# Gated recurrence of a mixer block: level factors as a tree of multiplied gates, paired value products, same-token term by head sums

## The reference: what is computed

```python
def step(S, inp):
    k_c, i_c, lf_c = inp[:3]
    g = jnp.cumsum(lf_c, axis=2)
    g_last = g[:, :, -1:, :]
    inter = jnp.einsum('bhtk,bhkv->bhtv', q_c * jnp.exp(g), S)
    rel = jnp.exp(jnp.where(causal, g[:, :, :, None, :] - g[:, :, None, :, :], -jnp.inf))
    scores = jnp.einsum('bhtk,bhsk,bhtsk->bhts', q_c, k_c, rel)
    o = inter + jnp.einsum('bhts,bhsv->bhtv', scores, i_c)
    S = (jnp.exp(g_last[:, :, 0, :])[..., None] * S
         + jnp.einsum('bhsk,bhsv->bhkv', k_c * jnp.exp(g_last - g), i_c))
    return S, o
```

## Time and profile before

| what | value |
|---|---|
| median of 3 runs | 5863.41 us (5860.79 to 5869.21) |
| the profiled execution, its own time | 5861.68 us |
| its span | 5859.9 us |
| granted TensorE clock, mean | 0.941 |
| busy: TensorE / VectorE / ScalarE / GpSimd | 5131.7 / 3377.3 / 1904.2 / 1745.5 us |

### The profile page before, as it was taken

One profiled execution on the slowest core, in us unless ns is written; L12 is line 12 of the kernel. 1 busy time (PEld: TensorE's weight loads), 2 busy tenths in 40 slices (PEclk: granted clock), 3 DMA queues, 4 the chain that ended last, 5 costly groups with the idle time before them and its releaser, 6 DMA issues. The chain is left out here.

```text
span 5859.9 us, 127569 instructions
## 1 busy us (share of the span) xinstructions
PE 5131.7 (88%) x55385; PEld 3930.2 (67%) x55385; DVE 3377.3 (58%) x5097; ACT 1904.2 (32%) x3020; POOL 1745.5 (30%) x1387
## 2 busy tenths in 40 slices
PE   6899999899995666587999868999988999989989
PEld 1588888788885555366888634444466788776667
DVE  2236656344444666576798257888864300058877
ACT  1234444233232443134211224444421300026652
POOL 2201111445453554034100005776743411100012
PEclk8999999899998888798999978999998999979999
DMA  5434434211112010464332421000055311230035
GB/s 200 124 107 163 150 135 152 95 56 60 60 52 90 23 58 27 159 215 146 96 108 94 164 101 41 17 17 23 14 176 160 99 68 69 78 127 39 32 116 165
DMA packets 430428, 568.20 MB, mean 97 GB/s; under 512 B 66918, under 2 KB 318694, under 8 KB 417214
## 3 DMA queue, kind: packets, MB, share of 16 engines
q1 hardware_dynamic: 362200, 380.35, 20.8%
q10 hardware_dynamic: 52470, 122.50, 5.5%
q0 software_dynamic: 15216, 57.44, 2.5%
HBM read 357.07 MB, written 203.12 MB: 96 GB/s over the span
## 5 line engine op out<-in xcount | busy, mean ns | idle before, releaser
L157 PE MATMUL p_bank<-p_hT_high,p_w_high 128*128 128x512 f32 (+1 forms) x2744 | 1037.0, 378 | 8.4 <-PEq L37 7.9
L159 PE MATMUL p_bank<-p_hT_high,p_w_low 128*128 128x512 f32 (+1 forms) x2744 | 1028.9, 375 | 0.0
L158 PE MATMUL p_bank<-p_hT_low,p_w_high 128*128 128x512 f32 (+1 forms) x2744 | 1028.7, 375 | 0.0
L157 PEld LDWEIGHTS p_bank<-p_hT_high,p_w_high 128*128 128x128 f32 x2744 | 517.0, 188 | 110.3 <-issue 17.6
L159 PEld LDWEIGHTS p_bank<-p_hT_high,p_w_low 128*128 128x128 f32 x2744 | 516.7, 188 | 93.7
L158 PEld LDWEIGHTS p_bank<-p_hT_low,p_w_high 128*128 128x128 f32 x2744 | 517.2, 188 | 91.4
L2902 POOL TENSOR_TENSOR at_acc<-at_acc,at_p 128x512 f32<-128x512 f32 x256 | 414.7, 1620 | 123.2 <-ACT at_p L2838 100.9
L2838 ACT ACTIVATE at_p<-at_sc 128x1024 f32<-128x1024 f32 (+1 forms) x296 | 284.5, 1012 | 377.6 <-PE at_sc L2729 368.9
L1560 PE MATMUL rsc_db<-rsc_W,rsc_TK 64*64 64x64 f32 x8640 | 383.1, 219 | 4.3 <-issue 3.8
L2944 DVE TENSOR_REDUCE at_mx<-at_mb 128x2 f32<-128x1024 f32 (+1 forms) x280 | 342.0, 1221 | 51.2 <-PE at_mb L2740 50.9
L157 PE MATMUL o_bank<-o_w_high,o_m_high 128*128 128x512 f32 x800 | 315.0, 394 | 62.6 <-POOL o_m_low L151 62.6
(11 more groups left out here) (433 smaller groups left out, 10575.0 us busy)
## 6 DMA issues: line engine op xcount, KB each, us to landing
rsc_X<-rwkv_chunks SPq DMA_DIRECT2D x108, 320.0 KB, 4.5
pT<-p_o ACTq DMA_DIRECT2D x128, 256.0 KB, 2.2
rwkv_chunks<-p_arr POOLq DMA_DIRECT2D x54, 512.0 KB, 5.3
o_z<-pT SPq DMA_DIRECT2D x50, 512.0 KB, 5.3
o_y<-y SPq DMA_DIRECT2D x50, 512.0 KB, 6.7
pT<-p_eo ACTq DMA_DIRECT2D x96, 256.0 KB, 2.0
x<-o_o ACTq DMA_DIRECT2D x32, 512.0 KB, 2.7
o_x<-x SPq DMA_DIRECT2D x32, 512.0 KB, 4.7
```

What stands on the lines that cost most here:

```text
L157: nc.tensor.matmul(out, lhs[0], rhs[0], start=start, stop=False)
L158: nc.tensor.matmul(out, lhs[0], rhs[1], start=False, stop=False)
L159: return nc.tensor.matmul(out, lhs[1], rhs[0], start=False, stop=stop)
```

## The change

It replaces running sums and their exponentials by products of gates. f = sigmoid(z) is the gate itself, `products(p, j)` the products of blocks of 2**j gates. The asks qe start as q times f and the keys ke as sigmoid(-z); at each level a copy of the later half of qe and of the earlier half of ke goes out to LVL (ScalarE), and then the same halves are multiplied in place by the product of the block that lies between (VectorE for asks, GpSimd for keys). After six levels qe and ke are the factors that the state term and the state need. Keys and values are turned three units ahead into one of five buffers, the values twice over, so that two levels' scores, side by side on 128 rows, meet the values in one product. The same-token term of both directions is v times the head sum of q times (k of direction 0 plus k of direction 1), made once per channel tile in the two context units of direction 1. The state term and the value products share one PSUM bank and one output operation. Gates are double-buffered, and the reset mask of the scan is not loaded any more. The diff, cut to its core (semaphore waits for reused buffers are left out in places):

```diff
-def hgrn(nc, PT, q0, i0, z0, seg, masks, ident, YH):
+def hgrn(nc, PT, q0, i0, z0, masks, ident, head_ones, YH):
...
-    MC = (LV + 1) * HD
+    LEAD, NK = 3, 5
+    PAIRS = LV // 2
+    MC = 2 * PAIRS * HD
...
-        KI = [s.sb(f"KI{u}", [P, 2, P]) for u in range(3)]
+        KI = [s.sb(f"KI{u}", [P, 3, P]) for u in range(NK)]
...
+        def side(a, j):
+            x = (a + j) % 2
+            return slice(x * HD, (x + 1) * HD)
+        def spot(a, j):
+            x = a * PAIRS + j // 2
+            return slice(x * HD, (x + 1) * HD)
...
             def _(pool):
+                def key_step(p, w, j):
+                    r = region(PHASES[p][1], w)
...
+                        pool.wait_ge(k_step[w], LV * p + j)
+                        pool.wait_ge(block_step, LV * p + j)
+                    if w < 2:
+                        pool.wait_ge(k_level[w], LV * p + j + 1)
+                    _, early = halves(ke[p % 2][:, r], 2 ** j, PHASES[p][1])
+                    nc.gpsimd.tensor_tensor(early, early, factors(p, j, r)[0], ALU.mult).then_inc(k_step[w], 1)
+                def same(p):
+                    m = PHASES[p][0]
+                    x = k[p % 2][:, 0:SEQ]
+                    pool.wait_ge(k_ready, p + 1)
+                    nc.gpsimd.tensor_tensor(x, x, k[1 - p % 2][:, 0:SEQ], ALU.add).then_inc(k_summed, 1)
+                    pool.wait_ge(k_summed, m + 1)
+                    nc.gpsimd.tensor_tensor(x, x, q[m % 2][:], ALU.mult).then_inc(same_ready, 1)
...
+                for p in range(NP):
                     for j in range(LV):
+                        key_step(p, 1, j)
                     if p + 1 < NP:
+                        for j in range(LV):
+                            key_step(p + 1, 2, j)
+                        if PHASES[p + 1][1]:
+                            same(p + 1)
+                        for j in range(LV):
+                            key_step(p + 1, 0, j)
...
             def _(act):
+                    nc.scalar.activation(ke[p % 2][:], f[p % 2][:], ACT.Sigmoid, scale=-1.0).then_inc(ke_raw, 1)
+                    nc.scalar.activation(k[p % 2][:, 0:SEQ], f[p % 2][:, 0:SEQ], ACT.Sigmoid, scale=-1.0).then_inc(k_ready, 1)
+                    nc.scalar.activation(f[p % 2][:], f[p % 2][:], ACT.Sigmoid).then_inc(f_ready, 1)
+                def level(p, w, j):
...
+                    nc.scalar.copy(early, keys).then_inc(k_level[w], 1)
+                    act.wait_ge(q_step[w], (LV + 1) * p + j + 1)
+                    nc.scalar.copy(late, asks).then_inc(q_level[w], 1)
...
                 for g in range(NU):
+                    if g + LEAD < NU:
+                        turned(g + LEAD)
+                    if unit(g)[4] < NLT and unit(g)[3] == 0:
+                        keep(g)
+                    if n < LV:
+                        level(p, 1, n)
                     if p + 1 < NP:
                         if n == 1:
+                            raw_keys(p + 1)
                         if n == 3:
+                            keep_keys(p + 1)
+                        if n == 4:
+                            gates(p + 1)
+                        if 9 <= n < 9 + LV:
+                            level(p + 1, 0, n - 9)
...
             def _(dve):
+                def blocks(p, j):
...
+                    nc.vector.tensor_tensor(out, late, early, ALU.mult).then_inc(block_step, 1)
+                def first_asks(p, w):
...
+                    nc.vector.tensor_tensor(qe[p % 2][:, r], q[m % 2][:, r], f[p % 2][:, r], ALU.mult).then_inc(q_step[w], 1)
+                def ask_step(p, w, j):
...
+                    nc.vector.tensor_tensor(late, late, factors(p, j, r)[1], ALU.mult).then_inc(q_step[w], 1)
...
+                    nc.vector.tensor_tensor(k[p % 2][:, t], yb[:, i % 2, :], v[m % 2][:, t], ALU.mult).then_inc(same_evac, 1)
...
+                    nc.vector.tensor_tensor(Y[w][:], Y[w][:], k[p % 2][:, w * HALF:(w + 1) * HALF], ALU.add).then_inc(same_added, 1)
...
                 for g in range(NU):
                     p, n = divmod(g, CH)
                     if g + 1 < NU:
                         state(g + 1, 0)
                         if unit(g + 1)[4] < NLT:
                             mask(g + 1)
                         state(g + 1, 1)
+                    if unit(g)[4] < NLT and unit(g)[3]:
+                        add(g)
+                    if unit(g)[3] and n < NCX:
+                        times_v(p, 2 * n)
+                        times_v(p, 2 * n + 1)
+                        add_same(p, n)
+                    if n < LV:
+                        ask_step(p, 1, n)
+                    if p + 1 < NP:
+                        if n == 6:
+                            for j in range(1, 3):
+                                blocks(p + 1, j)
+                        if n == 7:
+                            for j in range(3, LV + 1):
+                                blocks(p + 1, j)
+                            first_asks(p + 1, 0)
+                        if n == 8:
+                            first_asks(p + 1, 1)
+                        if 9 <= n < 9 + LV:
+                            ask_step(p + 1, 0, n - 9)
...
             def _(pe):
-                    nc.tensor.transpose(tb[:, 0, 0:P], ke[p % 2][:, t], idn[:])
-                    nc.tensor.transpose(tb[:, 1, 0:P], v[m % 2][:, t], idn[:]).then_inc(t_prod, 1)
+                    for a in range(2):
+                        chunk, ra = slice(c * P + a * HD, c * P + (a + 1) * HD), slice(a * HD, (a + 1) * HD)
+                        nc.tensor.matmul(tb[g % 2][ra, 0:P], ke[p % 2][:, chunk], idn[:], start=True, stop=True)
+                    for a in range(2):
+                        chunk = slice(c * P + a * HD, c * P + (a + 1) * HD)
+                        for x in range(2):
+                            last = nc.tensor.matmul(tb[g % 2][x * HD:(x + 1) * HD, (1 + a) * P:(2 + a) * P], v[m % 2][:, chunk], idn[:], start=True, stop=True)
...
+                            nc.tensor.matmul(yb[rh, a, 0:HD], S[(2 * g + i) % 6][rh, :], qe[p % 2][rh, t:t + HD], start=True, stop=False)
+                def back(g):
+                    pe.wait_ge(pr_ready, latents(g + 1))
+                    for i in range(PAIRS):
+                        for a in range(2):
+                            for h in range(2):
+                                rh = slice(h * HD, (h + 1) * HD)
+                                last = nc.tensor.matmul(yb[rh, a, 0:HD], KI[g % NK][:, 1 + a, rh], PR[g % 2][:, h, spot(a, 2 * i)],
+                                                        start=False, stop=(i + 1 == PAIRS))
...
+                    for h in range(2):
+                        rh = slice(h * HD, (h + 1) * HD)
+                        last = nc.tensor.matmul(yb[rh, i % 2, :], ones[:, rh], k[p % 2][:, i * NT:(i + 1) * NT], start=True, stop=True)
...
                 for g in range(NU):
-                    if g + 2 < NU:
-                        turn(g + 2)
                     if g + 1 < NU:
                         front(g + 1)
+                    if unit(g)[4] < NLT:
+                        asked(g)
+                    if g + LEAD < NU:
+                        turn(g + LEAD)
+                    if unit(g)[3] and unit(g)[1] < NCX:
+                        for i in range(2):
+                            same(unit(g)[0], 2 * unit(g)[1] + i)
                     if unit(g)[4] < NLT:
                         back(g)
```

379 lines of the change are left out of this document (161 added, 218 removed).

## The result

The changed kernel takes **5737.4 us** in the median of 4 runs (5732.4 to 5747.6), the kernel before 5866.3 beside it: ratio **0.9781 [0.9769, 0.9793]**, 2.2% faster. Forecast was 5764, range 5722 to 5822: the time is in the range, 27 us under the forecast.

What follows compares the result with a forecast made beforehand. TensorE was taken to be bound by instruction supply, 256 per 3.95 us. First value product at 1889 plus 371 us (units 96 x 3.4, seams 13 + 15 + 9 + 8) ends at 2260, 98.6 us less: 5764 us, range 5722 to 5822.

Steps and rivals of the forecast that it cites:

- Instruction supply bounds TensorE: Gated recurrence, kernel before: TensorE's instructions arrive in blocks of 256, one per 3.95 us; a unit costs 4.07 us.
- Supply still sets the pace, with little to spare: Changed kernel's latent units: a block takes 3.66 us of TensorE work against 3.95 us of supply.
- rival C: Units with a rung: ScalarE, GpSimd and VectorE form a chain, 72 units at 4.1 us, 50 us back, 5814 us; chance 0.14.
- The pace of a unit: Latent units of the stage: 3.4 us each, 96 units, from 3.13 by supply plus small waits; bounds 2.9 and 4.07.
- GpSimd's passes: Two 4.6 us GpSimd passes for the head sums hold VectorE's first asks: 3 us x 3 = 9 us.
- No gain of their own: Scan, masked exponentials and all but one table load, removed by the change: costed at no gain, being hidden.
- for shorter seams I take nothing: Granted clock, 0.50 over the start and 0.89 over the rest: no gain counted from shorter seams.
- Start: From the first loads to the first value product: it comes at 1889 instead of 1919.4, bounds 1886 to 1899.
- Seams: Five changes of phase: 13 us for context units, 15 for head sums, 9 for GpSimd passes, 8 for late gate loads.
- A: TensorE's stops belong to the unit, not the record count: pace 4.1, 67 us given back, 5831 us; chance 0.12.
- B: Supply is hidden with fewer records; pace is TensorE's own 2.9 us, 48 us less, 5716 us; chance 0.10.
- D: Units with a rung: the same chain wholly serial, 5.2 us a rung, 130 us given back, 5894 us, slower; chance 0.04.

Runs made afterwards that it cites:

- before_light: Kernel before, elementwise work preparing a phase cut to a sixteenth of its columns from the third phase on, all TensorE instructions kept: 5833.3 us, ratio 0.9940.
- before_lean: Kernel before with 12 of 28 value products of a unit left out, 215 TensorE instructions in place of 263: 5843.7 us, ratio 0.9962 to the kernel before.
- halved: Kernel after with each value product made in two of 32 columns, 251 instructions a unit: 5785.3 us, ratio 0.9865 to the kernel before.
- small_rungs: Kernel after with level work of GpSimd, VectorE and ScalarE cut to a sixteenth of its columns from the second phase on: 5710.3 us, ratio 0.9728.
- z_early: Kernel after with the gates of the next two phases loaded ahead of the output's stores: 5733.3 us, ratio 0.9777 to the kernel before.
- split_same: Kernel after with GpSimd's two 2048-column sums cut into eight 512-column operations between its key products: 5731.2 us, ratio 0.9768 to the kernel before.
- late_asks: Kernel after with VectorE's ask steps issued one unit later, ahead of the output's add: 5732.9 us, ratio 0.9774 to the kernel before.
- best1: Kernel after with split_same, z_early and late_asks together: 5734.2 us, ratio 0.9779 to the kernel before.
- filler: Kernel after with fifteen one-column products a unit added into unused columns, 263 instructions: 5823.1 us, ratio 0.9927 to the kernel before.

## Why the prediction was right, and where not

**Instruction supply bounds TensorE: right for the kernel before.** In the stretches where little else holds it, 256 instructions took 3.92 us (before, from restart to restart), 3.92 and 3.85 (before_light), 3.71 (before_lean, sixth phase), 3.93 (halved), 3.83 and 3.74 (small_rungs), and 3.81 between restarts of the kernel after and of small_rungs, whether a unit asks for 263, 251, 215 or 203. My 3.95 is the upper end of that.

**"Supply still sets the pace, with little to spare": wrong for the kernel after.** My sign for it, stops every 256 records, did not come: 5 stops with 5.8 us are left. "Issue" fell from 37.1 to 2.4 us at the scores because a unit asks for 203 instructions in place of 263, and at 3.23 us a unit that is one block in 4.07 us, slower than blocks come. What stands above the own unit of 2.71, 47 us in 90 intervals, is for the most part waits for VectorE and ScalarE (35.1 us in the table of waits, with those at the seams). VectorE is busy for 24.23 of the 26.64 us of the first window here. So 3.4 came near to the measured pace partly by luck: I had it from supply and small waits, and what holds the kernel after is closer to the chain of rival C, weaker than priced there. Windows of the kernel after, second and sixth phase:

```profile
1977.21:2003.85 26.64, 24.13 (x866) 22.35 (x864) 24.23 (x50) 10.31 (x20) 10.04 (x11) 1.00 0.07 24
2208.84:2234.74 25.90, 24.91 (x900) 23.21 (x898) 14.57 (x38) 3.83 (x8) 0.00 (x0) 1.00 0.07 24
```

3.94 and 3.69 us for 256; the first is not supply's, since no stop lies in that window. The Trainium skill (Runtime: NRT & Kernel Launch, section Instruction fetch mechanics) has fetch hidden; the 61 stops of the kernel before and the 22 of small_rungs, 16.5 us at 203 instructions a unit with next to nothing else to wait for, say that it is not hidden here.

**The pace of a unit: the term of the sum that was furthest off.** "Any wait over 0.3 us in a block now shows, so I take 3.4 us a unit instead of 3.13." Measured are 3.23 in the mean, with GpSimd's passes and late gates inside, which I had counted apart. Without them (16.2 us by the eighth and ninth intervals of the three phases of direction 0, 32.4 against 16.2 in small_rungs; 5.6 by z_early) it is 269 us over 90, 2.99 a unit. Waits and supply did not add up: while TensorE waits, blocks still arrive, and the next units run at 2.71 us from what lies ready. 90 x 0.41 = 37 us, the largest error of the sum. TensorE's own unit was 2.71, not 2.9: I had allowed 0.2 for semaphores that cost nothing, and two errors of 0.1 cancelled, 0.80 for scores that take 0.70 and 0.70 for values that take 0.80.

**"No gain of their own" for the scan and the exponentials: wrong as a reason.** before_lean shows that fewer instructions alone bring 24 us, and before_light that a lighter preparation alone brings 34. The forecast held because the change did both. I had read the busy shares (VectorE 67%, GpSimd 50%) as cover; what bound was a line through four engines, late by the end of each phase. The waits of the kernel before show it, from 1900 us on:

```profile
PE hg_tb L2087 <- ACT hg_KI L1922: 51.0, 19, 20.3
```

One wait of 20.3 us is of the start; of the other 30.7, nearly as much as the 37.1 of "issue" at the scores, I had priced 6.9 at the third phase. In before_light the seams gave 27 us.

**The clock "for shorter seams I take nothing": a term left out.** The granted clock rose from 0.89 to 0.97 behind the first value product. Its gain lies inside the paces and seams above, and how much of them it is stays open.

**Start: 34.1 us forecast from 1854.9, 38.3 measured.** From the true first load at 1852.4 the forecast was 36.6. Sigmoids were done 11.2 us after the first load (forecast 15.3). The first key product of 512 columns started 7.0 us behind them (forecast 4.6), because the tree of gates on VectorE took until 1878.2 and GpSimd's six context products 5.5 us. Six rungs took 11.7 us (forecast 12.0). From there to the first value product it was 8.3 us (forecast 4.5), TensorE busy for 8.30 of it, at a granted clock of 0.65 in the mean of this stretch.

**Seams: right in their sum.** 13 + 15 and five ordinary units of 3.4 make 45; measured 45.4. Their parts were not measured one by one. GpSimd's passes cost 16 us by the reckoning above, not 9, but split_same got back almost none of it: the price was of GpSimd's work, not of its long pieces. Late gates cost 5.6, not 8.

**The sum.** 37 (pace) less 10.7 (first value product at 1899.7 instead of 1889, 9.0 of it the later entry) less 7 (passes) plus 2.4 (gates) is 21.7 us better than forecast; the profiled time is 21 us under 5763. That the total came out so near is in part luck: its terms are off by 39 us one way and by 18 the other.

**Rivals.** A is out: the stops followed the count of instructions, in before_lean's sixth phase (57.1 to 44.9 us) most plainly. B was half true: supply is nearly hidden in the kernel after and single units run at 2.71, but the mean is not the own work, and it does not get there even in small_rungs (3.05), where the stops come back. C and D are out as prices, but their mechanism holds most of what stands above 2.71 in the kernel after. How it divides between GpSimd's hold on VectorE, VectorE's own work and ScalarE's queue stays open: split_same, late_asks and best1 each moved it and none removed it.

## What to carry to other kernels

When a wait for nothing ("issue") comes back in the middle of rows of equal products, count the instructions from one to the next; if the count is constant, fewer and larger products are worth more than faster ones. Count only steps that are longer than the products themselves, and compare the pace with the engine's own work before you call a bound shown: filler's time fitted the supply theory and was TensorE's own. Before pricing such a bound, look for the next one behind it: read a phase in which the other engines have nothing to prepare beside one in which they have. Here the two bounds gave 24 and 34 us alone, and the change that lifts both gave 101 behind the start. Moving a wait from where it shows does nothing if the engine that causes it has the same work to do.

## What the runs showed of the hardware that I had not expected

- Small float32 products had a price per record here, hardly one per column. Records of 128 rows took 33 ns a step at 64 columns; cutting them to 32 columns doubled their number at 29 ns each, and one-column records of 64 rows cost 34 ns. The 64 x 64 scores, four positions of the array in turn, took 14.6 ns a step. The Trainium skill (TensorE: Matmul & The Clock Gate, section Back-to-back issue gap) gives a floor of about 25 ns from start to start for products of up to 64 columns. A float32 product leaves two records here: the scores lie below that floor counted by record (14.6 ns) and above it counted by product (29 ns), all the others above it in both counts.
- A transpose of 128 x 128 and two products of 64 rows with the identity cost the same in the stream, 0.26 and 0.27 us to the next group's start; the values' turn behind it took 0.49 us to the next group's start instead of 0.44, so the own unit did not fall.
- A seam cost 13.3 to 14.5 us before (in the one to the third phase 3.8 of them are TensorE's wait for level products), 6.4 to 7.7 where the phase is prepared lightly in before_light, and 8.5 to 9.6 after.
